# Hybrid mixer layer: xbc pairs alternated with z and q pairs, all z tiles in pairs, one convolution of the sample columns, a key/value stage of its own

## The reference

```python
u = rmsnorm(x, norm_w)
proj = u @ w_in
cb, cc, ch, cz, sz, sxbc, sdt, mq, mz, gr = jnp.split(proj, idx, axis=-1)
conv_out, new_buf_a = causal_conv(cc * ch, buf_a, conv_a_w)
y_a = (jax.nn.silu(cz) * cb * conv_out) @ w_a_out
xbc, new_buf_s = causal_conv(sxbc, buf_s, conv_s_w, conv_s_b)
xbc = jax.nn.silu(xbc)
dt = jax.nn.softplus(sdt + dt_bias)
y, h_new = ssd_scan(xs, dt, a, bm, cm, h0)
...
k, v = jnp.split(rmsnorm(mem, mem_norm_w) @ w_mem_kv, 2, axis=-1)
s = jnp.einsum('bhld,bhmd->bhlm', q, k) / math.sqrt(256)
```

## Time and profile before

| what | us |
|---|---|
| median of three runs | 2257.66 (2257.50 to 2259.29) |
| the profiled execution | 2255.42 |
| its span in the trace | 2253.6 |
| PE busy | 2041.3 (91%) |
| DVE, POOL, ACT busy | 1289.1, 971.7, 741.4 |
| rows, norm and transposes | 0 to 64.6 |
| pairs | 64.6 to 865.0 |
| dt, z and key/value tiles | 865.0 to 1044.5 |
| transition | 1044.5 to 1072.4 |
| SSD stage | 1072.4 to 1656.4 |
| attention half 0 with output tiles | 1656.4 to 1790.6 |
| attention half 1 | 1790.6 to 1934.5 |
| output tiles, w_o and final rows | 1934.5 to 2253.6 |

### The profile page before, as it was taken

The page is one execution under the profiler, slowest core; times in us unless marked ns, Lnnn a source line. Parts: engine busy times, 40 slices in busy tenths (PEclk is TensorE's granted clock), DMA queues, the critical chain, the costliest instruction groups (busy, mean ns, idle before and its releaser), DMA issues.

```text
span 2253.6 us, 39463 instructions
## 1 busy us (share of the span) xinstructions
PE 2041.3 (91%) x13834; PEld 1947.5 (86%) x13834; DVE 1289.1 (57%) x2096; ACT 741.4 (33%) x1394; POOL 971.7 (43%) x613
## 2 busy tenths in 40 slices
PE   2788888899999999996999999999979989899998
PEld 2788888899999998996988988888869988799986
DVE  6577777644444112601788888888972345665343
ACT  6333333333333443111454555455531111201021
POOL 4666666677777673662313122222222221233700
PEclk9988999999999999998999999999989999999999
DMA  4122222212222224343656556564775586643421
GB/s 130 48 83 77 75 75 75 75 57 64 75 65 65 85 93 147 108 124 123 198 184 190 167 173 200 159 211 141 221 221 178 169 248 221 223 161 111 141 90 70
DMA packets 341061, 299.73 MB, mean 133 GB/s; under 512 B 21687, under 2 KB 304935, under 8 KB 339937
## 3 DMA queue, kind: packets, MB, share of 16 engines
q1 hardware_dynamic: 270994, 201.20, 29.8%
q10 hardware_dynamic: 70010, 97.80, 12.5%
HBM read 222.60 MB, written 76.59 MB: 133 GB/s over the span
## 4 chain that ended last, share of the span: by engine, by line
PE 54%; DVE 11%; DMA 7%; issue 6%; ACT 2%; SPq 1%; ACTq 1%; POOL 0%; DVEq 0%; POOLq 0%
PE acc L210 22%; PE pm L1711 16%; PE pm L1911 4%; PE acc L1711 4%; DMA arena<-s_qd 4%; PE pm L210 2%; DVE arena L1394 1%; DVE arena L1570 1%; PE pm L1812 1%; DVE arena L1440 1%; DVE arena L1393 1%; DMA out_s_ssm<-arena 1%; PE pm L1813 1%; PE pm L1810 1%; DVE arena L1437 1%
## 5 line engine op out<-in xcount | busy, mean ns | idle before, releaser
L210 PE MATMUL acc<-uhi,whi 128*128 128x344 f32 x1800 | 603.8, 335 | 42.2 <-POOL wlo L203 23.4
L210 PE MATMUL acc<-ulo,whi 128*128 128x344 f32 x1800 | 583.9, 324 | 0.0
L210 PE MATMUL acc<-uhi,wlo 128*128 128x344 f32 x1800 | 583.9, 324 | 0.0
L201 POOL TENSOR_SCALAR whi<-raw 128x1024 fp32r<-128x1024 f32 x91 | 118.1, 1298 | 882.5 <-DMA raw<-in_w_in 467.4
L730 POOL TENSOR_TENSOR blo<-wraw,bhi 128x512 fp32r<-128x512 f32 x210 | 296.1, 1410 | 234.7 <-ACT bhi L834 234.7
L210 PEld LDWEIGHTS acc<-uhi,whi 128*128 128x128 f32 x1800 | 347.5, 193 | 53.2 <-issue 52.9
L210 PEld LDWEIGHTS acc<-uhi,wlo 128*128 128x128 f32 x1800 | 346.6, 193 | 6.8 <-issue 6.0
L210 PEld LDWEIGHTS acc<-ulo,whi 128*128 128x128 f32 x1800 | 346.4, 192 | 0.0
L1711 PE MATMUL pm<-uhi,bhi 128*128 128x258 f32 x704 | 211.6, 301 | 69.9 <-DVE room L1226 58.5
L203 POOL TENSOR_TENSOR wlo<-raw,whi 128x1024 fp32r<-128x1024 f32 x91 | 255.4, 2807 | 7.6
L1711 PE MATMUL pm<-shi,bhi 128*128 128x258 f32 x832 | 236.1, 284 | 2.2 <-ACT psb L872 2.2
(11 more groups left out here) (302 smaller groups left out, 3992.4 us busy)
## 6 DMA issues: line engine op xcount, KB each, us to landing
wraw<-in_w_in SPq DMA_DIRECT2D x70, 512.0 KB, 4.7
raw<-in_w_in SPq DMA_DIRECT2D x43, 512.0 KB, 5.0
stage<-s_g SPq DMA_DIRECT2D x32, 516.0 KB, 5.5
arena<-s_cs SPq DMA_DIRECT2D x32, 512.0 KB, 5.1
s_xbc<-room ACTq DMA_DIRECT2D x24, 516.0 KB, 2.6
s_g<-stage ACTq DMA_DIRECT2D x24, 516.0 KB, 2.8
raw<-in_w_mem_kv SPq DMA_DIRECT2D x16, 512.0 KB, 3.8
arena<-s_xbc SPq DMA_DIRECT2D x32, 256.0 KB, 4.6
```

The source lines that it names most:

```text
L201: pool.tensor_scalar(whi[r][:], raw[r][:], 1.0, 0.0, ALU.mult, ALU.add).then_inc(w_high[r], 1)
L210: mm = pe.matmul(out, w[r][:, k, :], a[:, k, c0:c0 + n], start=k == 0 and s == 0, stop=k == KT - 1 and s == 2)
```

## The change

- Flat pairs: 12 instead of 7, all sixteen z tiles in eight and the q tiles in four. For twelve turns an xbc pair is followed by a flat one; then the 16 pairs of the first branch. 40 pairs.
- DVE's order in such a turn: additions of the xbc pair, four taps of tile 1, the flat pair's first additions, two taps of tile 0, its other additions, the last two taps (`xbc_and_flat`). Only the 1024 prompt columns go through the taps.
- The flat results stay in p1, p5, u2 and `corner`, get their silu or scale there, and go out in five DMAs a pair; `keep` waits for f_saved before it writes these buffers again.
- The sample columns of all 24 tiles are convolved at once behind the pairs (`tips`, eight DVE operations and one of ACT); their two loads from s_xbc go.
- The dense z tiles go. The key/value stage is sixteen products on three weight slots and three PSUM banks; ACT makes the high parts of the weights (`high_w`), POOL the low ones (`low_w`). The loads of the memory rows wait for the last stores of both kinds.
- Attention half 1: queries in two sets of buffers, keys in two halves, each loaded when the four reads of its half are done; the first keys and two sets of queries are loaded in half 0.
- Some semaphores are merged, and SP's waits for `stored` ahead of the SSD stage go.

```diff
...
-XP, CP, FP = XT // 2, 2 * KT, 7
+XP, CP, FP = XT // 2, 2 * KT, XT // 2
+ZP, V1 = ZT // 2, XT // 2
...
+kv_tile = lambda i, j: (i + (j == 0), j, None)
...
+tips = hist_s[:, :, :, :].rearrange("p t b k -> p (t b k)")[:, 0:XT * NB].rearrange("p (t b) -> p t b", b=NB)
+dec_x, bcx = tips[:, 0:ZT, :], tips[:, ZT:, :]
+tip_sum = room[:, 0:XT * NB].rearrange("p (t b) -> p t b", b=NB)
+corner = (toks[:, 0:QC], usum[:, 0:QC])
...
+q_even = [dq[:, h * MD:(h + 1) * MD] for h in range(MH)]
+q_odd = [hist_q[:, 0:MD], hist_q[:, MD:2 * MD], cs_tok[:, :], dt_tok[:, :]]
+q_heads = (q_even, q_odd)
+Q_PARTS = (((dq, 0, KT),), ((hist_q[:, 0:2 * MD], 0, 4), (cs_tok[:, :], 4, 2), (dt_tok[:, :], 6, 2)))
...
+    for lo, hi, srcs in ((1, ZP, z_srcs), (ZP, V1, q_srcs)):
+        with sp.Fori(lo, hi) as v:
+            next_pair(v, 0, xbc_srcs(v))
+            next_pair(v, 1, srcs(v))
...
     sp.wait_ge(multiplied, 2 * NJ * PAIRS)
...
-        load_w(sp, z_first[n], w_in[:, :, O_SZ + n * P:O_SZ + (n + 1) * P])
...
-        sp.wait_ge(c_saved[b], 16 * (XP + 3 + (KT if b else 0)))
+        sp.wait_ge(c_saved[n], 16 * (XP + (KT if n else 0)))
+    for i, s in enumerate(f_saved):
+        sp.wait_ge(s, 16 * FP * (2 if i == 3 else 1))
...
-    with sp.Fori(0, 4) as i:
-        for j in range(6):
-            load_w(sp, mixed_tile(i, j), kv_src(kv_of(i, j)) if j % 3 else z_src(z_of(i, j)))
+    with sp.Fori(0, 5) as i:
+        for j in range(3):
+            load_w(sp, kv_tile(i, j), kv_src(i * 3 + j))
...
-        sp.dma_start(dec_x, s_xbc[0:INNER, SEQ:].rearrange("(t p) b -> p t b", p=P)).then_inc(dec_in, 16)
...
-    split_pair(PAIRS // 2, 0)
...
-    pool.wait_ge(multiplied, 2 * NJ * PAIRS)
-    for t in z_first:
-        split_w(pool, t)
-    with pool.Fori(0, 4) as i:
-        for j in range(6):
-            split_w(pool, mixed_tile(i, j))
+    def low_w(t):
+        pool.wait_ge(w_high[t[1]], t[0] + 1)
+        pool.tensor_tensor(wlo[t[1]][:], raw[t[1]][:], whi[t[1]][:].bitcast(F32), ALU.subtract).then_inc(w_split[t[1]], 1)
...
+    KEEP = {0: (p1, 0, 1, 0), 2: (u2, 0, 5, 2), 3: (p5, 2, 3, 1)}
+    def keep(v, b, j, freed):
+        dst, s_of, read_at, save_of = KEEP[j]
+        if freed is not None:
+            act.wait_ge(f_saved[save_of], freed)
...
+    def silu_xbc(v, n):
+        act.wait_ge(conv, v * 10 + (5 if n else 10))
+        act.activation(cv[n][:, 0:SEQ], cv[n][:, 0:SEQ], ACT.Silu).then_inc(silu_done, 1)
+        save(cv[n][:, 0:SEQ], rows(s_xbc, v * 2 + n)[:, 0:SEQ], silu_done, v * 5 + (2 if n else 5), c_saved[n])
...
+    def flat_part(v, i, z):
+        dst, func, scale, t0 = flat_to[z]
+        buf, n, cols = ((p1, 0, LEFT), (p5, 1, RIGHT), (u2, 1, LEFT))[i]
+        act.wait_ge(added, v * 12 + (6 + ADDED + 2 * i + 2))
+        act.activation(buf, buf, func, scale=scale).then_inc(silu_done, 1)
+        save(buf, rows(dst, v * 2 + (n - t0))[:, cols], silu_done, v * 5 + (1, 3, 4)[i], f_saved[i])
+    def flat_last(v, z, opening=False):
+        dst, func, scale, t0 = flat_to[z]
+        if not opening:
+            act.wait_ge(f_saved[3], v * 32)
+        last_out(v, 1, corner, func, scale)
+        act.wait_ge(kept, v * 16 + (8 + KEPT + 8))
+        for q in range(2):
+            act.dma_start(rows(dst, v * 2 - t0)[:, HC + q * QC:HC + (q + 1) * QC], corner[q]).then_inc(f_saved[3], 16)
+    late = lambda v, z: {0: [lambda: flat_part(v, 2, z)], 2: [lambda: silu_xbc(v, 0)]}
+    def flat_pair(v, z, opening=False):
+        act_pair(v, 1, lambda: flat_last(v, z, opening),
+                 {2: [lambda: flat_part(v, 0, z)], 3: [lambda: silu_xbc(v, 1)], 5: [lambda: flat_part(v, 1, z)]})
...
+    with act.Fori(1, ZP) as v:
+        act_pair(v, 0, lambda: xbc_last(v), late(v - 1, True), freed=v * 16)
+        flat_pair(v, True)
...
+    save_a(c)
+    act.wait_ge(tip_step, 8)
+    act.activation(tips, tip_sum, ACT.Silu).then_inc(tip_step, 1)
...
-    to_dram(act, z_first[0], 0, s_z[0:P, :], ACT.Silu)
...
-    to_dram(act, z_first[1], 0, s_z[P:2 * P, :], ACT.Silu)
...
-    act.dma_start(bcx, s_xbc[INNER:, SEQ:].rearrange("(t p) b -> p t b", p=P)).then_inc(bcx_in, 16)
+    def high_w(t):
+        act.wait_ge(w_loaded[t[1]], (t[0] + 1) * 16)
+        act.wait_ge(done[t[1]], t[0] + OPEN)
+        act.activation(whi[t[1]][:], raw[t[1]][:], ACT.Copy).then_inc(w_high[t[1]], 1)
+    def keep_kv(t, n):
+        act.wait_ge(done[t[1]], t[0] + 1 + OPEN)
+        act.activation(kv_t[:, bass.ds(n, 1), :].rearrange("p a m -> p (a m)"), pm[2 + t[1]][:, 0:NM],
+                       ACT.Copy).then_inc(kv_evac[t[1]], 1)
+    for j in range(3):
+        high_w(kv_tile(0, j))
     act.wait_ge(u_low, 8 * STEPS + 2 * (NM // P))
...
+        for j in range(3):
+            keep_kv(kv_tile(i, j), i * 3 + j)
+            high_w(kv_tile(i + 1, j))
...
-    def load_sample(k):
-        act.wait_ge(S["sam_read"], k * 8 + OPEN)
...
+    def load_queries(k, b, first=False):
+        if not first:
+            act.wait_ge(S["sam_read"], k * 8 - 8 + OPEN)
+            settle(act)
+        for dst, t, n in Q_PARTS[b]:
+            act.dma_start(dst.rearrange("p (t n) -> p t n", n=P),
+                          s_qd.rearrange("(t b) n -> b t n", b=NB)[bass.ds(k, 1), t:t + n].to_broadcast([P, n, P])).then_inc(landed[b], 16)
+    def load_keys(k, b, first=False):
+        for a in range(2):
+            if not first:
+                act.wait_ge(S["sam_read"], k * 8 + (4 * a - 4) + OPEN)
+                settle(act)
+            act.dma_start(dk[:, a:a + 1, :],
+                          I["cache_mem_k"][0, bass.ds(k, 1)].rearrange("c (a m) h d -> m (c a) (h d)", m=P)[:, a:a + 1, :]).then_inc(landed[b], 16)
...
+    load_keys(0, 0, first=True)
+    load_queries(0, 0, first=True)
+    load_queries(1, 1, first=True)
...
-    act.wait_ge(S["q_saved"], 16)
...
-        load_sample(i * 2)
         exp_scores(i, 1)
         copy_probs(i, 1)
-        load_sample(i * 2 + 1)
+        load_keys(i * 2 + 1, 1)
+        load_queries(i * 2 + 2, 0)
         save_att(i, 1)
-    load_sample(6)
+        load_keys(i * 2 + 2, 0)
+        load_queries(i * 2 + 3, 1)
...
-    load_sample(7)
+    load_keys(7, 1)
...
-    def conv_xbc(v, b, n, opening=False):
...
+    def conv_tap(v, n, k):
+        j, c0 = v * 2 + n, v * 10 + (0 if n else 5)
+        x, y, w = xp[n], cv[n], col(C_SW + k * XT, v * 2 + n)
+        if k == 0:
+            dve.tensor_copy(tail_s[:, bass.ds(j, 1), :].rearrange("p a b -> p (a b)"), x[:, SEQ:]).then_inc(conv, 1)
+            dve.tensor_scalar(y[:, 0:SEQ], x[:, 0:SEQ], w, col(C_SB, j), ALU.mult, ALU.add).then_inc(conv, 1)
+            return
+        dve.wait_ge(conv, c0 + (1 + k))
+        dve.scalar_tensor_tensor(y[:, 0:SEQ], x[:, k:k + SEQ], w, y[:, 0:SEQ], ALU.mult, ALU.add).then_inc(conv, 1)
+    def xbc_and_flat(v, opening=False):
         if not opening:
-            dve.wait_ge(c_saved[n], v * 32 + b * 16)
-        dve.tensor_copy(tail_s[:, bass.ds(j, 1), :].rearrange("p a b -> p (a b)"), x[:, SEQ:]).then_inc(conv, 1)
+            dve.wait_ge(conv, v * 10)
+        add_pair(v, 0, xp[0][:, KS - 1:], xp[1][:, KS - 1:])
+        dve.wait_ge(added, v * 12 + (ADDED + 6))
+        if not opening:
+            dve.wait_ge(c_saved[1], v * 16)
         for k in range(KS):
-            now = x[:, SEQ + KS - 1:] if k == KS - 1 else hist[:, :, k]
...
-    def xbc_pair(v, b, opening=False):
+            conv_tap(v, 1, k)
+        add(v, 1, 1, p1)
+        all_added(v, 0)
         if not opening:
-            dve.wait_ge(conv, v * 36 + b * 18)
-        add_pair(v, b, xp[0][:, KS - 1:], xp[1][:, KS - 1:])
-        all_added(v, b)
-        conv_xbc(v, b, 1, opening)
-        conv_xbc(v, b, 0, opening)
-    xbc_pair(0, 0, True)
-    xbc_pair(0, 1)
-    with dve.Fori(1, XP // 2) as v:
-        xbc_pair(v, 0)
-        xbc_pair(v, 1)
-    V1 = XP // 2
+            dve.wait_ge(c_saved[0], v * 16)
+        for k in range(2):
+            conv_tap(v, 0, k)
+        add(v, 1, 4, p5)
+        add(v, 1, 5, u2)
+        for k in range(2, KS):
+            conv_tap(v, 0, k)
...
+    tip_w = lambda k: par[:, C_SW + k * XT:C_SW + (k + 1) * XT]
+    for k in range(KS - 1):
+        dve.tensor_tensor(hist_s[:, :, :, k], hist_s[:, :, :, k], bcast(tip_w(k), NB), ALU.mult).then_inc(tip_step, 1)
+    dve.tensor_tensor(tip_sum, tail_s[:, :, KS - 1:], bcast(tip_w(KS - 1), NB), ALU.mult).then_inc(tip_step, 1)
+    dve.wait_ge(tip_step, 4)
+    for k in range(KS):
+        more = hist_s[:, :, :, k] if k < KS - 1 else bcast(par[:, C_SB:C_SB + XT], NB)
+        dve.tensor_tensor(tip_sum, tip_sum, more, ALU.add).then_inc(tip_step, 1)
+        dve.wait_ge(tip_step, 5 + k)
...
+    def sample_scores(i, b):
+        k = i * 2 + b
+        if b:
+            dve.wait_ge(S["sam_odd"], (i + 1) * 80)
+        else:
+            dve.wait_ge(S["sam_even"], (i + 1) * 48)
...
-    pair_product(PAIRS // 2, 0)
...
-    dense(pe, z_first[0])
...
-    dense(pe, z_first[1])
...
-    with pe.Fori(0, 4) as i:
```

(60 more changed lines are left out.)

221 lines of the change are left out of this document (74 added, 147 removed).

## The result

The changed kernel takes 2142.86 us (median of four runs, 2135.09 to 2143.99) against 2257.65 before: a ratio of 0.949, 95% interval 0.947 to 0.951. The forecast was 2155, its range 2135 to 2183. The profiled execution is 2143.95 us with a span of 2141.8, 111.8 us shorter than the span before.

| stage | before | after | difference | forecast |
|---|---|---|---|---|
| start | 64.6 | 64.8 | +0.2 | 0 |
| pairs (35, then 40) | 800.5 | 812.0 | +11.5 | +11.5 |
| key/value stage | 179.4 | 78.1 | -101.3 | -95.5 |
| transition | 27.9 | 27.6 | -0.3 | -0.4 |
| SSD and attention half 0 | 718.2 | 721.3 | +3.1 | 0 |

A forecast was written before the change was run, and what follows sets the result against it. PE was taken as the bound, stalled by DVE's convolutions in xbc pairs, by dense tiles, and by sample loads in half 1. 2255.4 + 11.5 - 95.5 - 0.4 - 18 = 2153, forecast 2155 us, range 2135 to 2183.

The forecast's parts named there:

- Pairs: Pair stage: 39 pairs after the opening one at 20.15 us each, DVE having two pairs' time for one's work; +11.5 us.
- rival (4): Pair stage: alternation keeps the stall, held by DVE's order or ACT's new waits; +171 us, 2326 us, chance 2%.
- Sample columns: Pair stage: 96 small DVE operations go, eight for all tiles come behind the pairs; nothing, bounds 0 to +2 us.
- Key/value stage: Between pairs and transition, without ten z tiles: E + 84 instead of 179.5 us, -95.5; E is the end of the pairs.
- My stretch of the chain: Key/value stage: DVE's dt chain, 39.4 us before, lengthened by 1.5 to 59 us beside busier POOL, ending at E + 83.5.
- Weight high parts on ACT: Key/value stage: rounding moved to ACT costs nothing; 21 us if no slot ran ahead.
- Attention half 1: Attention half 1: of 22.3 us of stalls, both placed ones and half of the other 8.0 go; -18 us.
- Both stalls that I placed: Attention half 1: ACT's queue 6.11 us on issuing first keys, PE idle 8.19 us for splitting the next activations; both go.
- Rival (3): Attention half 1: loads are bound by DMA, so stalls move but don't go; +18 us, 2173 us, chance 11%.
- Rival (1): Key/value stage runs at the lower clock; +27 us, 2182 us, chance 12% together with chain and low parts not overlapping.
- Rival (2): Pair stage: ACT held at f_saved costs PE a microsecond per cycle; +11 us, 2166 us, chance 12%.
- Stages left alone: SSD, attention half 0 with its new early loads: no change; a move of over 5 us would show the prediction wrong.

## Why the prediction held, point by point

- **What bounds the kernel.** Right in each stage: the stall of the xbc pairs, PE in the dense z tiles, the sample loads in half 1.
- **Pairs.** The term was +11.5, measured +11.5: 20.15 us a pair, all 39. In the chain of work of the changed kernel the same piece starts 40.29 us apart, two pairs on, here among the alternating pairs:

```profile
177.46 23.01 PE pm L1742 x192
217.75 23.01 PE pm L1742 x192
```

The twelve slowed pairs that I counted as xbc pairs are eleven of these and the first pair of the first branch, which stood behind the last convolution and its store; the sum is the same.

The sum was right, its reason only in part. In the kernel before DVE had 21.7 us of work for a pair of 20.15, and the alternation gave it two pairs for that: so far the reason by amount holds. But I dismissed rival (4) with DVE's 18.9 of 40.3 us. With the same amount and another order a stall was back (+66.9 us, by way of ACT), and with a larger amount in the new order it was not. What carries the step is the sentence on the written order, that no addition queues behind more than four taps. The rival's mechanism is real, its price was too high (5.6 us a turn of two pairs, not 7.45 a pair), and the changed kernel avoids it.
- **Sample columns.** Nothing, as said: put back, the small operations cost nothing (2142.58 us).
- **Key/value stage.** 78.1 us instead of 84, the term that was most off (-101.3 for -95.5). The loads were asked for at E + 6.5 (forecast E + 6.3). The chain began at E + 22.75, 2 us early: I kept the 2.03 and 3.23 us that the two normalisations took beside POOL, and POOL now rests then. Another wait ends last there now: ACT works on dt until 896.5 and splits the rows right behind it (L987).

```profile
895.42 1.07 ACT L980 ACTIVATE arena<-arena 32x1032 f32<-32x1032 f32 x1
896.48 2.20 ACT L987 ACTIVATE mhi<-pm 128x512 fp32r<-128x512 f32 x4
```

The chain took 55.4 us, not 59; low parts 3.25 us, not 3.5. That both ends lie together was right: the chain ended 0.93 us after PE's last product. My stretch of the chain was not the mechanism, and that its size came near is in part luck: I spread one factor of 1.5, from POOL's share of busy time, over the whole chain. In turns the eight steps went from 14.91 / 8 = 1.86 us in the kernel before to 3.34, 1.8 times, while the reciprocal (6.59 us) and the scan (2.28 us) took what they had taken.

```profile
910.53 14.91 DVE L1349 SCALAR_TENSOR_TENSOR arena<-arena 32x1032 f32<-32x1032 f32 x8
```

The rule of the Trainium skill, "SBUF — State Buffer", section "Who interferes with whom", that the two engines exclude each other, agrees with these rows: a step beside a low part takes 3.34 us, near the sum of 1.22 and 2.39, and halving the low part cut it to 2.23.
- **Weight high parts on ACT.** Nothing, as said: ACT was busy 32.5 of 78.1 us and PE waited for the low parts.
- **Attention half 1.** -22.7 for -18. Both stalls that I placed went, and all of the other 8 us, of which I took half. Rival (3), loads bound by DMA, falls: the same bytes, but for the first keys and two sets of queries, came in 121.2 us at a share of 0.85 (254 GB/s) with PE never idle.
- **Rival (1)**, the lower clock in the key/value stage, did not come: PE's pauses between products were 0.3 us at most, and the next matmuls ran at 0.28 us. Only the first product, behind a pause of 4.59 us, ran its first half at 0.41 us a matmul, near the 0.42 that the earlier trace rows has at the lower clock.

```profile
902.63 0.58 PE L211 MATMUL pm<-mhi,whi 128*128 128x256 f32 x1 [4.59 <-POOL wlo L790]
903.01 0.41 PE L211 MATMUL pm<-mhi,wlo 128*128 128x256 f32 x1
931.44 0.38 PE L211 MATMUL pm<-mhi,whi 128*128 128x256 f32 x1 [0.29 <-POOL wlo L790]
931.66 0.28 PE L211 MATMUL pm<-mhi,wlo 128*128 128x256 f32 x1
```

The swings that the Trainium skill describes in "TensorE: Matmul & The Clock Gate", section "A second HAM failure mode: psum-queue depth-cycling", are not seen between these products.

- **Rival (2)**, ACT held at f_saved, came about without a price: ACT waits 2.07 us for a store in the turn shown, and PE, busy all through the stage, does not notice.

```profile
280.93 0.66 ACT L875 ACTIVATE psb<-pm 128x258 f32<-128x258 f32 x2 [2.07 <-DMA s_z<-psb]
```

- **Stages left alone.** SSD and half 0 show +3.1 and the rest -2.2. SSD, counted up to the first score product of half 0, took 591.8 us before and 593.4 after, and half 0 from there 126.4 and 127.9. In the ten profiled executions here of the changed kernel and its variants SSD took 589.9 to 596.0 us and half 0 125.6 to 128.2, so the +3.1 is within the spread of executions. The last part took 313.8 to 317.1 us in these ten, and 319.1 and 318.5 in the kernel before and the one without its sample columns; so the -2.2 need not be spread, and its cause was not looked for, nor what makes SSD vary.

## What to carry to other kernels

When an engine off the critical path feeds the one on it, its share of busy time says only whether the work can fit; whether it does is decided by where, in its written order, the small operations that others wait for stand among the large ones, and by who queues behind them on a third engine. Before pricing an engine's step from a trace, look at what ran beside it, and price it again for what will. A load issued on an engine's own queue costs that engine its issue time, and here its place in the order counted more than its bytes: the same six issues took 5.3 us in half 0 and 17.9 us in half 1.
